# A pipelined end of the mixer, single-pass routing products, low parts on VectorE and ten gather buffers in a two-layer mixer and MoE kernel

## The reference

```python
for layer in range(2):
    xn = rmsnorm(h, mix_norm_g)
    proj = xn @ w_in                      # q,f,i,g of HGRN2; q,k,v and indexer of DSA; two gates
    y_a = hgrn2_mixer(...)                # gated linear recurrence, 4 heads of 128
    y_b = dsa_mixer(...)                  # indexer picks 132 keys a query, softmax attention, 8 heads
    h = h + (sigmoid(gate_a) * (y_a @ w_branch_hgrn) + sigmoid(gate_b) * (y_b @ w_branch_dsa)) @ w_out
    # hierarchical MoE: top-1 of 4 groups, then top-2 of its 8 experts, renormalised weights
    xn = rmsnorm(h, ffn_norm_g)
    h = h + sum over the two chosen experts of w_e * ((silu(xn @ gate_e) * (xn @ up_e)) @ down_e)
return rmsnorm(h, final_norm_g)[:, 16:]
```

## Time and profile before

| | |
|---|---|
| runs | 1929.77, 1930.25, 1931.74 us; median 1930.25 |
| profiled execution | 1931.6 us, span 1929.7 us |
| granted TensorE clock, mean | 0.872 of full speed |
| busy in the span | PE 79%, PEld 61%, DVE 36%, ACT 30%, POOL 20% |
| DMA | 342.48 MB, mean 177 GB/s; in the expert stages 365 to 384 GB/s |
| chain that ended last | PE 34%, issue 24%, SP's queue 18%, DVE 8%, DMA 7%, POOL 6% |

### The profile page before, as it was taken

How to read it: one execution, slowest core, us unless ns; L and a number is a source line. 1 busy time by engine, 2 the same in 40 slices (tenths; PEclk the granted TensorE clock), 3 DMA queues, 4 the chain that set the end, 5 groups by cost and what they waited for, 6 DMA issues and landing times.

```text
span 1929.7 us, 31682 instructions
## 1 busy us (share of the span) xinstructions
PE 1526.8 (79%) x11236; PEld 1175.7 (61%) x11236; DVE 700.0 (36%) x1678; ACT 575.4 (30%) x990; POOL 382.2 (20%) x237
## 2 busy tenths in 40 slices
PE   2999876979988499877449998678898975987771
PEld 1768876966857355444237698677767763554440
DVE  4136978035332311011241399751354132111114
ACT  4234443255412011111223355334453120111111
POOL 6303240210420011000143043213005101110002
PEclk9998986989987599899679889779899967999995
DMA  4211250111335499999831122202114356999994
GB/s 163 88 44 44 89 220 13 56 56 61 132 148 213 149 365 368 380 379 377 284 115 44 45 88 86 93 19 93 35 50 167 139 219 229 369 369 377 387 384 161
DMA packets 97702, 342.48 MB, mean 177 GB/s; under 512 B 12528, under 2 KB 12912, under 8 KB 80416
## 3 DMA queue, kind: packets, MB, share of 16 engines
q1 hardware_dynamic: 71152, 274.38, 38.7%
q0 software_dynamic: 9344, 33.95, 5.6%
q10 hardware_dynamic: 17072, 32.39, 4.6%
HBM read 302.49 MB, written 38.21 MB: 177 GB/s over the span
## 4 chain that ended last, share of the span: by engine, by line
PE 34%; issue 24%; SPq 18%; DVE 8%; DMA 7%; POOL 6%; ACT 2%; ACTq 0%; DVEq 0%; POOLq 0%
SPq L519 11%; PE ps L677 10%; SPq L525 7%; PE ps L654 6%; POOL gate_up_low L1920 5%; PE ps L940 4%; PE ps L664 3%; PE ps L961 2%; PE ps L866 2%; DMA expert<-w_expert_up 1%; PE ps L898 1%; DMA r<-yrow,sidx 1%; DMA gu_ring<-w_expert_up 1%; PE ps L841 1%; PE ps L859 1%
## 5 line engine op out<-in xcount | busy, mean ns | idle before, releaser
L1920 POOL TENSOR_TENSOR gate_up_low<-gu_ring,chunk_high_a 128x1024 fp32r<-128x1024 f32 x80 | 195.2, 2458 | 477.6 <-ACT chunk_high_a L1605 477.6
L677 PE MATMUL ps<-x_high,chunk_high_a 128*128 128x264 f32 x896 | 269.8, 301 | 18.3 <-POOL gate_up_low L1920 13.8
L677 PE MATMUL ps<-x_high,gate_up_low 128*128 128x264 f32 (+1 forms) x928 | 275.8, 297 | 0.0
L677 PE MATMUL ps<-x_low,chunk_high_a 128*128 128x264 f32 x896 | 265.4, 296 | 0.0
L677 PEld LDWEIGHTS ps<-x_high,chunk_high_a 128*128 128x128 f32 x896 | 180.6, 202 | 23.4 <-issue 23.0
L1978 POOL DMA_INDIRECT r<-xrow,idx x64 | 57.0, 890 | 647.1 <-PE ps L929 443.4
L677 PEld LDWEIGHTS ps<-x_high,gate_up_low 128*128 128x128 f32 (+1 forms) x928 | 184.6, 199 | 0.6
L677 PEld LDWEIGHTS ps<-x_low,chunk_high_a 128*128 128x128 f32 x896 | 180.7, 202 | 0.0
L654 PE MATMUL ps<-gate_up_low,x_high 128*128 128x512 f32 (+1 forms) x400 | 162.7, 407 | 0.0
L1507 DVE COPY r<-ps 128x512 f32<-128x512 f32 x64 | 44.3, 691 | 277.2 <-PE ps L929 277.2
L1920 POOL TENSOR_TENSOR gate_up_low<-gu_ring,chunk_high_b 128x1024 fp32r<-128x1024 f32 (+1 forms) x26 | 58.6, 2280 | 282.8 <-ACT chunk_high_b L1605 282.6
(11 more groups left out here) (309 smaller groups left out, 2964.7 us busy)
## 6 DMA issues: line engine op xcount, KB each, us to landing
gu_ring<-w_in SPq DMA_DIRECT2D x20, 2048.0 KB, 9.1
gu_ring<-w_expert_gate SPq DMA_DIRECT2D x22, 1024.0 KB, 26.7
gu_ring<-w_expert_up SPq DMA_DIRECT2D x22, 1024.0 KB, 25.6
dn_ring<-w_expert_down SPq DMA_DIRECT2D x44, 512.0 KB, 25.2
r<-w_expert_down SPq DMA_DIRECT2D x40, 512.0 KB, 25.8
yrow<-r ACTq DMA_DIRECT2D x128, 128.0 KB, 7.2
expert<-w_expert_gate SPq DMA_DIRECT2D x12, 1024.0 KB, 26.6
expert<-w_expert_up SPq DMA_DIRECT2D x12, 1024.0 KB, 27.2
```

What stands on the lines that cost most here:

```text
L677: last = mm(o[:, lo:hi], w[:, c, quarter(name, j)], x[:, c, lo:hi], start=c == 0 and k == 0, stop=c == KC - 1 and k == 2)
L1920: G.tensor_tensor(low[:, :, cols], w[:, :, cols], high[:, :, cols].bitcast(F32), ALU.subtract).then_inc(sem["part_low"], 1)
```

## The change

- The order of the end of the mixer comes from a new function `output_order`, used by TensorE, VectorE, ScalarE and the job list: the first four tiles of half 0, four of half 1, then the last tile of each. Transposes of tile k follow the output tile after the one that completes it, and its router product one tile later.
- The root of the mean square is taken for each tile (`row_rms(i)`), and VectorE normalises tile by tile (`norm_row`), at the start of a layer and in front of the router.
- The products of `rank` and `slot` have float32r operands. Two constant matrices are rounded once at the start.
- VectorE makes the low parts of k3, k2, hf, wo0 and wo1; GpSimd keeps the others. The counter `part_low` becomes `low_v` and `low_p`.
- h is written to `hrow` by SyncE's queue, ahead of the load of k1.
- The combine has ten gather buffers, four in r1 and six in the place of an expert buffer, and GpSimd waits for none.

```diff
+VSPLIT = ("k3", "k2", "hf", "wo0", "wo1")
+def output_order():
+    done = []
+    for half, i in [(0, 0), (0, 1), (0, 2), (0, 3), (1, 0), (1, 1), (1, 2), (1, 3), (0, 4), (1, 4)]:
+        yield ("wo", half, i)
+        if half == 0 and i < 4:
+            continue
+        done.append((half, i))
+        k = len(done) - 2
+        if k >= 1:
+            yield ("ro", k - 1)
+        if k >= 0:
+            yield ("xt2", k)
+    yield ("ro", NT - 1)
...
-    last["wo0"] = add(*[("wo", 0, i) for i in range(NT)])
-    last["wo1"] = add(*[("wo", 1, i) for i in range(NT)])
-    add(("xt2", 0), ("xt2", 1))
-    for i in range(2, NT):
-        add(("ro", i - 2), ("xt2", i))
-    last["ro"] = add(("ro", NT - 2), ("ro", NT - 1))
+    last["ro"] = add(*output_order())
+    last["wo0"], last["wo1"] = (jobs.index(("wo", half, NT - 1)) for half in range(2))
...
-        yg = r1[:, 0:4096].rearrange("p (u n) -> p u n", u=4)
+        yg = [r1[:, k * D:(k + 1) * D] for k in range(4)]
+        yg += [expert0[:, k * D:(k + 1) * D] for k in range(6)]
...
 # SyncE
+                    if name == "k1":
+                        for i in range(NT):
+                            sp.wait_ge(*at("cb_done", 2 * (i + 1) - 2 * NT))
+                            sp.dma_start(hrow[T0[i]:T0[i] + TS[i], :], h[0:TS[i], i, :]).then_inc(sem["h_out"], 16)
...
 # TensorE
-                for half in range(2):
-                    token_major(f"wo{half}", 512, ml, ("wo", half))
-                norm_transposes("xt2", NT, router)
-                router(NT - 2)
-                router(NT - 1)
+                for job in output_order():
+                    if job[0] == "wo":
+                        token_major(f"wo{job[1]}", 512, ml, ("wo", job[1]), (job[2],))
+                    elif job[0] == "xt2":
+                        norm_transposes("xt2", NT, job[1])
+                    else:
+                        router(job[1])
...
-                        last = mm(s[...], lhs[0:TS[k], :], Cs[0:TS[k], k, :], start=True, stop=True)
+                        last = mm(s[...], counters[0:TS[k], m, :], Csr[0:TS[k], k, :], start=True, stop=True)
...
 # VectorE
+                def low_part(name, q):
+                    dve.wait_ge(*at("part_high", UNITS[name, q] + 1))
+                    tt(low[:, :, cols], w[:, :, cols], high[:, :, cols].bitcast(F32), ALU.subtract).then_inc(sem["low_v"], 1)
+                def norm_row(k0, i):
+                    dve.wait_ge(*at("rms_ready", k0 + i + 1))
+                    link(V.reciprocal(rstd[:, i:i + 1], rms[:, i:i + 1]))
+                    if i >= 2:
+                        done(("xt2" if k0 else "xt", i - 2))
+                        if k0:
+                            dve.wait_ge(*at(f"xw{i % 2}", 16 * (i // 2)))
+                    stt(xn[0:n, i % 2, :], h[0:n, i, :], rstd[0:n, i:i + 1], gB[0:n, :], ALU.mult, ALU.mult)
-                norm_rows(0)
+                low_part("k3", 0)
+                for i in range(NT):
+                    norm_row(0, i)
+                    if i < 4:
+                        low_part("k2", i)
...
                     for hd in range(IH):
+                        if i == NT - 1 and hd % 2 == 0:
+                            low_part("hf", hd // 2)
                         index_score(i, hd)
...
 # in the loop over the eight blocks of wb
                     if c > 0:
                         merged_low(c - 1)
+                    if c % 2:
+                        low_part("wo0", c // 2)
...
+                for job in output_order():
+                    i = job[-1]
+                    if job[0] == "wo":
+                        tt(o, job_slab(job)[0:n, 0:512], o, ALU.add).then_inc(*free(job))
+                        if half == 0 and i < 4:
+                            low_part("wo1", i)
+                    elif job[0] == "xt2":
+                        norm_row(NT, i)
+                    else:
+                        logits(i)
...
 # ScalarE
+                def row_rms(i):
+                    link(A(pr[0:n, 2048:3072], h[0:n, i, :], ACT.Square, accum_out=ss[0:n, i:i + 1]))
+                    A(rms[:, i:i + 1], ss[:, i:i + 1], ACT.Sqrt, scale=1.0 / D, bias=eps_t).then_inc(sem["rms_ready"], 1)
...
 # GpSimd, combine
                 for k in range(2 * NT):
-                    if k >= 4:
-                        pool.wait_ge(*at("cb_done", k - 3))
-                    pool.indirect_dma_start(yg[0:n, k % 4, :], None, yrow, ...)
+                    pool.indirect_dma_start(yg[k][0:n, :], None, yrow, ...)
```

More of the change, by code:

```diff
@@ L628, in chunk, with norm_transposes @@
                     return gu_ring[:, n % 2, :]
-                def norm_transposes(job, k0, then=None):
-                    for i in range(NT):
-                        if then and i >= 2:
-                            then(i - 2)
-                        s = take((job, i))
-                        pe.wait_ge(*at("xn_ready", k0 + i + 1))
-                        settle(pe)
-                        for c in range(KC):
-                            last = tr(s[:, c * P:c * P + TS[i]], xn[0:TS[i], i % 2, c:D:KC], ident[0:TS[i], 0:TS[i]])
-                        last.then_inc(sem["pe_done"], 1)
+                def norm_transposes(job, k0, i):
+                    s = take((job, i))
+                    pe.wait_ge(*at("xn_ready", k0 + i + 1))
+                    settle(pe)
+                    for c in range(KC):
+                        last = tr(s[:, c * P:c * P + TS[i]], xn[0:TS[i], i % 2, c:D:KC], ident[0:TS[i], 0:TS[i]])
+                    last.then_inc(sem["pe_done"], 1)
                 def low_parts(name, q):
-                    pe.wait_ge(*at("part_low", UNITS[name, q] + 1))
+                    pe.wait_ge(*at(*LOW[name, q]))
                 def token_major(name, n, x_low, job, tiles=range(NT)):
@@ L1402, in _ @@
                 settle(dve)
-                for half in range(2):
-                    for i in range(NT):
-                        n = TS[i]
-                        done(("wo", half, i))
-                        o = h[0:n, i, half * 512:(half + 1) * 512]
-                        tt(o, job_slab(("wo", half, i))[0:n, 0:512], o, ALU.add).then_inc(*free(("wo", half, i)))
                 def logits(i):
@@ L1612, in _ @@
                     high_part(name, q)
-                row_rms("mix_norm_g")
+                load_scale("mix_norm_g")
+                for i in range(NT):
+                    act.wait_ge(*at("cb_done", 2 * (i + 1) - 2 * NT))
+                    row_rms(i)
                 for i in range(NT):
@@ L1960, in _ @@
                     low_part("gb0", q)
[L1962 to L1968 removed]
+                for q in range(4):
+                    if q in (1, 2):
+                        for c in ((0, 1) if q == 1 else (2, 3)):
+                            pool.wait_ge(*at("yh_ready", c + 1))
+                            G.tensor_tensor(yl[:, c, :], ybT[:, c, :], yh[:, c, :].bitcast(F32), ALU.subtract).then_inc(sem["yl_ready"], 1)
+                    low_part("wb", q)
                 pool.wait_ge(*at("xw0", 48))
```

131 lines of the change are left out of this document (64 added, 67 removed).

## The result

The changed kernel takes 1917.91 us (median of 4 runs, 1916.08 to 1920.71); the kernel before, run beside it, 1930.99 us. The ratio is 0.993, interval 0.9911 to 0.9949: 13 us faster, where 34 were forecast, and 6 us above the upper end of the forecast's range. The profiled execution took 1920.7 us, with a span of 1919.1.

The account below looks back on a forecast made before the run. DMA weight streaming bounds the expert stages, with serial mixer and router ahead. Gains of 17.5 us in layer 0 and 16.4 in layer 1, together 33.9, gave a forecast of 1896 us, range 1886 to 1906.

Parts of the forecast that it names:

- What bounds the kernel: Whole kernel: DMA sets the expert stage's end, so time won before the first expert shifts the whole weight stream.
- End of the mixer: Output tiles to last logits: interleaved order listed step by step to 82.8 us, gaining 7.0 in layer 0, 5.6 in layer 1.
- Rival 3: Output tiles: clock falls behind five gaps of 2 us, 33 us a layer, 1963 in all; chance 0.04.
- 3 (gaps cost the clock once): Mixer end: lower bound of the gain per layer, 3 us; the upper bound was 9.
- Rivals 1 and 2: 1: square and root in different tables, two loads per row, 1907, chance 0.07. 2: expert stream does not move, 1917, 0.07.
- Rival 4: Low parts cost VectorE as much and disturb nothing less: hf 0, wo0 -4, k2 -1 a layer; 1912, chance 0.05.
- with rivals 1 and 4: The forecast's range widened to include these two rivals: 1884 to 1912 us.
- Index scores: VectorE's index operations with hf's low parts moved there: 13.9 to 11.0 us, gain 2.9 in each layer, bounds 0 to 4.
- Start of layer: Row scalings with k3 and k2 low parts on VectorE: gain 0.5 us in layer 0, 1.9 in layer 1.
- Rank and slot: Single-pass products after the router: rank gains 3.0 us, slot 0.9, 3.9 a layer, bounds 2.5 to 4.3.
- Combine: Ten gather buffers remove GpSimd's waits: gain 2.8 us in layer 0, 1.7 in layer 1.
- wo0's parts: wb loop: moving wo0's low parts to VectorE gains a net 0.4 us a layer, bounds -3 to 1.

Follow-up runs that it names:

- the kernels with the serial end: Changed kernel with the old order (ten output tiles, then transposes and router), 1899.7 us; the same with all low parts back on GpSimd, 1909.7 us.
- the other trace of the changed kernel: The changed kernel run once more with no edit: 1914.3 us.
- thirty products: The 1856.2 us kernel with 30 in place of 18 unused products ahead of wo0's last low part: 1856.2 us.

## Why the prediction was wrong, step by step

- **What bounds the kernel.** Right within 3 us. What is won ahead of the first expert comes out at the end, in the change and in all experiments: the expert stage (expert 0's to 31's gate-up copy) is 258 to 264 us in all of them, 259.9 and 259.1 before, 262.4 and 259.8 in the changed kernel.
- **End of the mixer: the step that failed.** The list put the last logits 82.8 us behind the first output product; they came 92.95 behind it. Against its own marks: row 0's transposes start at 41.0 (38.2 forecast), row 1's end at 54.0 (48.1), row 3's at 74.8 (68.5), the last tile at 82.0 (74.0), the last transposes start at 86.0 (78.2). Two things make the 10.1 us. First, "this wait comes with rows 1, 2, 3" left out row 0, for which VectorE stands behind the add of the next tile in the same way: 2.25. (Rival 3 counts this wait: it has five gaps, the list four.) Second, "Transposes now at full clock" and tiles of 5.55 priced no wait by what it does to the clock: 1.7 in the pair behind the first wait, 2.8 in the tile behind row 0, 1.6 in the last, 2.3 in the last transposes and router, 8.4 in all. Small pieces add 0.6, and the first four tiles were 1.2 faster than forecast. The bound "3 (gaps cost the clock once)" excluded what happened. With the clock held by unused products the stage is 85.0, which is about the forecast plus row 0's wait; with the waits themselves removed it is 75.8, 14 and 12 less than before.
- **Rival 3** had the mechanism, and the chance of 0.04 was the real error. I asked whether the clock would fall for whole tiles (5.55 each, half of the tiles), and found that unlikely. It falls for part of a tile (1.6 to 2.8): too little to make the kernel slower, which was all I had asked, and enough to take the gain. The evidence against it, full clock at 7.16 busy of 10 us in the earlier trace rows, was read from one window and not from the stage. The idle time in it is one piece of 2.84 us, and the trace of the kernel before has eleven pieces of 2.6 to 3.5 us in the expert stage of layer 0. Behind eight of them the granted clock of the next 5 us is 0.50 to 0.72, behind three 1.00; the window of the earlier trace rows has one of the three. TensorE's timeline, the same 32 products behind two of these waits, with 0.66 and 1.00:

```profile
834.65 5.36 PE L940 MATMUL ps<-r 128*64 128x256 f32 x32 [3.09 <-DMA r<-w_expert_up]
853.90 3.67 PE L940 MATMUL ps<-pr,r 128*64 128x256 f32 x32 [2.84 <-DMA pr<-w_expert_up]
```

  Inside the expert stage this costs nothing, since DMA sets its end. But it was there to be seen what a wait of 2 to 3 us does to the products behind it: 1.7 us in 3.7, and not each time.
- **Rivals 1 and 2 are out.** No table load stands at a square behind a root: five pairs run with one load, at the first root (24.33 and 575.00 us in layer 0). The prediction's "none ahead of a square or a copy" was misread, since the kernel before has two ahead of a copy (14.39 and 953.05 us), near the start of each layer; it changes nothing here. The Trainium skill, "ScalarE: Activation LUTs", section "Table sets: the hidden batching unit", asks for activations batched by table set and leaves open whether the root's set has the square; here the pair repeats without a load, so the rule costs nothing. And the queue was empty before routing ended: expert loads 1 to 4 moved as listed, a little later (610, 622 and 633 us for 607, 617 and 626), and the DMA share was 0.01 between 647 and 652 us. **Rival 4** as a whole is out too, though it is right that the low parts gain nothing at the start of a layer. Its own figures add up to 1915, not to the 1912 that it states, so the range "with rivals 1 and 4" should have ended at 1915; 1917.9 is outside that too.
- **Index scores.** Right in kind, too small: 4.8 for 2.9. "With four low parts of 1.18 between: 11.0" counted one too many: the first is made while VectorE waits for ScalarE anyway (158.51 is the first index operation, and three low parts follow). That is 1.2; the first operation takes 0.49 and not 0.80, and a low part adds 1.05. Together 9.15. The Trainium skill, "SBUF — State Buffer", section "Who interferes with whom", says that a VectorE instruction with two inputs in SBUF shares a port with a GpSimd one that reads SBUF, and not with one that only writes. The traces agree: 3.2 to 3.4 us in place of 1.28 beside low parts, 1.26 beside clearing (three in 3.77). The first index operation has only one such input and was slowed as well, 2.19 for 0.49 us.
- **Start of layer.** 2.45 and 4.4 for 0.5 and 1.9. The step "VectorE is back from the loop branch 4.2 us after the last combine" was wrong: before, 2.8 of the 4.2 us were a square, a table load of 1.28 and the root of all rows at once, which ended 1.4 us ahead of VectorE's reciprocal; with a root for each row the load comes with the first and the wait is 1.77, in the row at 974.18. The low parts themselves brought nothing, and cost 4.1 us in layer 1 by where they stood (19.2 against 15.1 to the last x_low).
- **Rank and slot.** 2.25 and 1.1 for 3.0 and 0.9. Ten single-pass products took 2.61 us at half clock (granted 0.50), above my upper end of 2.4, so VectorE still waits 1.04. With TensorE kept busy they take 1.58, at 1.00.
- **Combine.** 0.8 for 2.8 in layer 0 (first gather to last add 23.67 and 22.87), 2.6 for 1.7 in layer 1. The ten gathers go out without a wait, as forecast; "copies of h now run among them" was named and thought to be within the 2.8; with the copies late the gain is 3 us, with the copies among the gathers 0.8.
- **wo0's parts.** In the whole stretch from the selection to wb's end they can't be told from noise of up to 5 us. In the wb loop itself, from VectorE's first add to the last low part of the merged branches, it is 27.8 and 27.7 us before and 27.1 and 26.9 after, and 27.3 and 27.5 against 26.7 and 26.8 in the kernels with the serial end: 0.6 to 0.9 us for the forecast's 0.4.

Not settled: in layer 0 the first gather leaves 7.75 us behind the start of the last y copy in place of 5.86 (8.8 in the other trace of the changed kernel), and expert 0's first transposes start 1.2 us later behind the copy of the indices (10.5 for 9.3). No run was made on these.

## What to carry to other kernels

A wait on the matmul engine has two prices: itself, and the clock behind it. When an order adds waits of 2 us between long products, price each with a half-clock stretch (here 1.6 to 2.8 us of a 5.6 us tile, behind three waits of five), and let the engine that feeds it do the feeding operation first; that alone took 28 us off the two stages here, where the new order of the products had added 15 to the serial one. Before calling such a fall unlikely, look at the granted clock behind every wait of that length in the trace at hand, not in one window. Work that is put on a faster engine counts by its place: behind what others wait for, not between.

## What the runs showed of the hardware

- TensorE's granted clock fell to half after idle stretches of only 2.0 to 2.3 us, but not after each of them: behind the wait of 1.84 at 592.79 and that of 2.01 at 603.21 the tile took 5.57. It also fell behind an idle stretch of 1.11 us (thirty products, layer 1, 1496.40), where the same stretch in layer 0 cost nothing.
- Unused products of 128x128 by 128 take 0.23 us each at full clock (24 in 5.6 us). Thirty that ended 0.9 and 0.4 us ahead of the real work held the clock for it; 18 that ended 3.5 and 3.9 us ahead of it did not.
- With TensorE busy without a break the granted clock still differs between traces with the same instructions there, 0.66 against 1.00 over 10 us, 4.3 us in a stage of 120.
- Float32r products of 128 rows by 32 columns took 0.26 us each at half clock and 0.16 at full, where float32 ones took 0.49 at half: 1.9 times less, where the kernel's description has one pass for four.
